# Keeping the weight chunks of the first token group in memory as they lie in their slots

## The reference

```
h  = rmsnorm(x) * g_mix
z  = h @ w_in                     # 512 pool | 512 q | 128 k | 128 v | 1024 gate_pool | 1024 gate_attn
A  = per-group map of (windowed mean - identity) of the pool part, scaled
B  = attention (8 heads, 2 kv heads, q and k normalised and rotated)
x += (sigmoid(gate_pool) * (A @ w_pool_out) + sigmoid(gate_attn) * (B @ w_attn_out)) @ w_out
h  = rmsnorm(x) * g_ffn
q  = h @ w_query                  # 8 heads, two halves of 128 each
s  = q . sub_keys                 # 128 scores per half; the best 16 of each half, merged to the best 16 pairs
x += sum over 8 heads x 16 experts of gelu(h . expert_u[id]) * gate * expert_v[id]
y  = rmsnorm(x) * g_final
```

## Time and profile before

| | |
|---|---|
| median of 3 runs | 2869.37 us (2869.11 to 2872.34) |
| the profiled execution: time, span | 2890.73 us, 2888.9 us |
| TensorE busy | 2606.0 us, 90% |
| VectorE busy | 2087.9 us, 72% |
| GpSimd busy | 1591.7 us, 55% |
| DMA moved | 965.76 MB, mean 334 GB/s |
| of it by gathers / by SP's queue | 671.17 MB / 261.61 MB |
| mean granted TensorE clock | 0.964 |

### The profile page before, as it was taken

The page is one execution under the profiler, slowest core; times in us unless marked ns, Lnnn a source line. Parts: engine busy times, 40 slices in busy tenths (PEclk is TensorE's granted clock), DMA queues, the critical chain, the costliest instruction groups (busy, mean ns, idle before and its releaser), DMA issues.

```text
span 2888.9 us, 30850 instructions
## 1 busy us (share of the span) xinstructions
PE 2606.0 (90%) x9957; PEld 1549.0 (54%) x9957; DVE 2087.9 (72%) x4622; ACT 538.5 (19%) x1205; POOL 1591.7 (55%) x1284
## 2 busy tenths in 40 slices
PE   7999958999798977999579999899999999999998
PEld 6867836885234455555344444455444545444454
DVE  1232987768707867788789987977777778777785
ACT  2141132221008104444430000010000000100001
POOL 0000165345765765344447877787777667666672
PEclk9999979999999989999899999999999999999999
DMA  4324599997898898899989999999999999999994
GB/s 160 103 84 131 200 328 338 388 326 260 324 372 289 299 368 290 281 346 311 328 311 405 412 376 414 411 376 412 413 413 413 414 413 413 414 413 413 410 410 190
DMA packets 345125, 965.76 MB, mean 334 GB/s; under 512 B 26018, under 2 KB 152738, under 8 KB 326306
## 3 DMA queue, kind: packets, MB, share of 16 engines
q0 software_dynamic: 184320, 671.17, 60.7%
q1 hardware_dynamic: 108800, 261.61, 24.2%
q10 hardware_dynamic: 51872, 31.46, 3.5%
HBM read 932.68 MB, written 31.46 MB: 334 GB/s over the span
## 4 chain that ended last, share of the span: by engine, by line
PE 32%; DMA 26%; DVE 22%; issue 12%; POOL 4%; ACT 3%; another core or an unknown queue 1%; DVEq 0%; ACTq 0%; POOLq 0%
DMA ring<-in_expert_v,idx 13%; PE bank L674 12%; DMA ring<-in_expert_u,idx 9%; PE bank L662 9%; DVE ring L1389 6%; POOL ring L1354 3%; PE bank L952 3%; PE o_bank L942 2%; PE o_bank L694 2%; DVE h L1389 2%; PE bank L733 2%; DVE region_c L1389 1%; DVE consts L1807 1%; DVE consts L1801 1%; DMA region_c<-in_expert_u,idx 1%
## 5 line engine op out<-in xcount | busy, mean ns | idle before, releaser
L1354 POOL DMA_INDIRECT ring<-in_expert_u,idx x468 | 608.3, 1300 | 667.3 <-DVE idx L1692 294.5
L952 PE MATMUL bank<-wslot,gate_attn 128*128 128x512 f32 x1536 | 697.8, 605 | 59.5 <-DVE gate_attn L1741 59.4
L1354 POOL DMA_INDIRECT ring<-in_expert_v,idx x428 | 507.5, 1186 | 323.2 <-issue 116.9
L942 PE MATMUL o_bank<-region_a,wslot 128*128 128x384 f32 x2048 | 681.3, 486 | 0.0
L942 PEld LDWEIGHTS o_bank<-region_a,wslot 128*128 128x128 f32 x2048 | 389.0, 190 | 298.0 <-issue 60.3
L952 PEld LDWEIGHTS bank<-wslot,gate_attn 128*128 128x128 f32 x1536 | 294.2, 193 | 420.5 <-issue 322.5
L1389 DVE CUSTOM_DVE_ANT_0 ring<-ring,h 128x1024 f32<-128x1024 f32 x380 | 451.5, 1222 | 48.4 <-DMA ring<-in_expert_u,idx 45.8
L1406 DVE SCALAR_TENSOR_TENSOR region_b<-ring,dots,region_b 128x1024 f32<-128x1024 f32 x256 | 328.6, 1283 | 120.8 <-DMA ring<-in_expert_v,idx 98.5
L1260 ACT ACTIVATE gate_attn<-o_bank 128x384 f32<-128x384 f32 x128 | 62.9, 491 | 1282.8 <-PE o_bank L942 1251.8
L674 PE MATMUL bank<-region_b,wslot 128*128 128x256 f32 (+1 forms) x768 | 231.6, 460 | 1.6 <-ACT region_b L989 1.6
L674 PE MATMUL bank<-region_a,wslot 128*128 128x256 f32 (+1 forms) x768 | 229.4, 457 | 2.9 <-DMA wslot<-in_w_in 1.7
(11 more groups left out here) (215 smaller groups left out, 2898.2 us busy)
## 6 DMA issues: line engine op xcount, KB each, us to landing
wslot<-in_expert_uT SPq DMA_DIRECT2D x64, 1024.0 KB
wslot<-in_expert_v SPq DMA_DIRECT2D x64, 1024.0 KB
wslot<-in_w_in SPq DMA_DIRECT2D x34, 1024.0 KB
wslot<-in_w_query SPq DMA_DIRECT2D x24, 1024.0 KB
expert_weights<-region_p ACTq DMA_DIRECT2D x24, 1024.0 KB
wslot<-in_w_out SPq DMA_DIRECT2D x12, 1024.0 KB
region_s<-expert_weights SPq DMA_DIRECT2D x8, 1536.0 KB
region_p<-expert_weights SPq DMA_DIRECT2D x8, 1536.0 KB, 12.8
```

The lines of the kernel that those rows point to most:

```text
L942: ins = nc.tensor.matmul(dense_in[q][:, 0:DENSE_T], u_cols[slot][:, k, :], mergeds[1][:, k, T - DENSE_T:T], start=(k == 0), stop=(k == KD ...
L952: ins = nc.tensor.matmul(dense_out[2 * t + n][:], hidden[q][:, t * P:(t + 1) * P], v_cols[slot][:, n * 512:(n + 1) * 512], start=start, st ...
L1354: nc.gpsimd.indirect_dma_start(ring_row(n), None, expert_u if what == "u" else expert_v, bass.IndirectOffsetOnAxis(ap=ids, axis=0)).then_i ...
```

## The change

Each of group 0's 29 chunks is stored to a DRAM tensor, `kept_dram`, from its slot, once it has landed there. The store of chunk m - 3 is issued on SP's queue right behind the load of chunk m (`STORE_BEHIND` is 3). The load that overwrites a slot (chunk m, where chunk m - 4 is of group 0) waits for that store too. The 53 chunks of groups 1 and 2 are loaded from `kept_dram`, where one partition's 8 KB lie in one run; their attn_out chunks take one DMA in place of two. `chunk_landed` counts accordingly and is moved up in the code. Nothing else is altered.

```diff
+KEPT = {chunk[1:]: n for n, chunk in enumerate(chunk_order(0))}
+STORE_BEHIND = WSLOTS - 1
...
+        kept_dram = nc.dram_tensor("kept_weights", (len(KEPT), P, KD * CHUNK), F32, kind="Internal").ap()
...
+        w_stored = sems("w_stored", WSLOTS)
...
+                count += 2 if n < len(KEPT) and CHUNKS[n][1] == "attn_out" else 1
...
+            def load_chunk(chunk):
+
+                m, name, c = CHUNKS.index(chunk), chunk[1], (chunk[2] if len(chunk) > 2 else 0)
+                dst, loaded = wslot[:, m % WSLOTS, :], w_loaded[m % WSLOTS]
+                if chunk[0]:
+                    sp.dma_start(dst, kept_dram[KEPT[chunk[1:]]]).then_inc(loaded, 16)
+                elif name in w_in_cols:
...
+            def keep_chunk(m):
+
+                chunk_landed(sp, CHUNKS[m])
+                sp.dma_start(kept_dram[m], wslot[:, m % WSLOTS, :]).then_inc(w_stored[m % WSLOTS], 16)
...
                     if m >= WSLOTS:
                         filled(sp, *LAST_JOB[CHUNKS[m - WSLOTS]])
+                        if m - WSLOTS < len(KEPT):
+                            sp.wait_ge(w_stored[m % WSLOTS], 16 * ((m - WSLOTS) // WSLOTS + 1))
...
+                    load_chunk(chunk)
...
+                    if STORE_BEHIND <= m < len(KEPT) + STORE_BEHIND:
+                        keep_chunk(m - STORE_BEHIND)
                     if name == "out" and c == 1 and g != LAST_GROUP[0]:
                         load_residual(g)
```

More of the change, by code:

```diff
@@ L504, in all_used, with chunk_landed @@
                 used(eng, n)
+        def chunk_landed(eng, chunk):
+            m = CHUNKS.index(chunk)
+            count = 0
+            for n in range(m % WSLOTS, m + 1, WSLOTS):
+                count += 2 if n < len(KEPT) and CHUNKS[n][1] == "attn_out" else 1
+            eng.wait_ge(w_loaded[m % WSLOTS], 16 * count)
+            return m % WSLOTS
         block = ctx.enter_context(nc.Block())
@@ L525, in load_residual @@
                                  res_loaded, 16)
+            w_in_cols = {"p": 0, "q": POOL_W, "kv": POOL_W + Q_W, "gate_pool": POOL_W + QKV_W,
+                         "gate_attn": POOL_W + QKV_W + D}
+            def load_chunk(chunk):
[4 more added lines that the diff above has]
+                elif name in w_in_cols:
+                    at0 = w_in_cols[name] + c * CHUNK
+                    sp.dma_start(dst.rearrange("p (k n) -> p k n", k=KD),
+                                 w_in[:, at0:at0 + CHUNK].rearrange("(k p) n -> p k n", p=P)).then_inc(loaded, 16)
+                elif name == "pool_out":
+                    sp.dma_start(dst.rearrange("p (g n) -> p g n", g=GROUPS),
+                                 w_pool_out[:, c * 512:(c + 1) * 512].rearrange("(g p) n -> p g n", p=P)).then_inc(
+                                     loaded, 16)
+                elif name == "attn_out":
+                    dst = dst.rearrange("p (j n) -> p j n", j=PAIRS)
+                    for half in range(KV_HEADS):
+                        src = w_attn_out[half * PAIRS * HD:(half + 1) * PAIRS * HD,
+                                         c * 512:(c + 1) * 512].rearrange("(j p) n -> p j n", p=HD)
+                        sp.dma_start(dst[half * HD:(half + 1) * HD], src).then_inc(loaded, 16)
+                else:
+                    w = w_out if name == "out" else w_query
+                    sp.dma_start(dst.rearrange("p (k n) -> p k n", k=KD),
+                                 w[:, c * CHUNK:(c + 1) * CHUNK].rearrange("(k p) n -> p k n", p=P)).then_inc(loaded, 16)
+            def keep_chunk(m):
+                chunk_landed(sp, CHUNKS[m])
+                sp.dma_start(kept_dram[m], wslot[:, m % WSLOTS, :]).then_inc(w_stored[m % WSLOTS], 16)
             load_x(0)
@@ L529, in _ @@
             sp.dma_start(g_mix_sb[:], g_mix).then_inc(first_loaded, 16)
-            w_in_cols = {"p": 0, "q": POOL_W, "kv": POOL_W + Q_W, "gate_pool": POOL_W + QKV_W,
-                         "gate_attn": POOL_W + QKV_W + D}
             for g in range(len(GROUP_OF)):
@@ L624, in encoder_kernel @@
         FIRST_ALL, CONSTS_ALL = 2 * 16, 7 * 16
[L626 to L633, removed]
         @block.tensor
```

## The result

The changed kernel takes 2885.15 us (median of 6 runs, 2876.84 to 2888.61), the kernel before on the same chip 2870.86. One of the six executions of the kernel before took 5476.58 us; it is in this median and left out of the ratio. The ratio is 1.0048, with an interval of 1.0032 to 1.0064: 0.48% slower, about 14 us. Forecast were 2861 us and 0.28% faster.

What follows compares the result with a forecast made beforehand. TensorE was taken to bound the untouched last stage, half the time; gathers and VectorE's dots mattered earlier. Gains 1.5 + 4.8 + 0.6 + 1.0 + 0 + 0 = 7.9 us gave 2861 us, range 2856 to 2866 (8 in 10: 2846 to 2878).

Steps and rivals of the forecast that it cites:

- part 4: Group 0's 29 stores: 73 us of DMA time, mostly under an idle stretch, expected to cost 0.
- one turn: SP's chain in group 0 from load to next load: 7.9 us, 8.3 with keys, at most 9.7, against 9.1.
- the rival that I gave 9%: Slower by the stores: group 0's turn exceeds 9.1 us; at 10 us group 0 ends 14 us later, 2876; chance 9%.
- Part 1: Shorter DMA time of the 53 loads: a gather before group 1's attention comes 1.5 us earlier, bounds 0 and 2.4.
- part 2: Group 1's late chunks: waits around the first out chunk go; 4.8 us, then 0.6 and 1.0.
- two gathers' worth: Before group 1's out, loads draw about 1.2 MB forward, against 8 ring slots, so VectorE's dots don't get later.
- slower by the gathers: Loads' larger share delays gathers 1.6 us each; nine chunks in group 2 cost 14 us, giving 2876; chance 8%.
- The 0.6: In group 1, the wait for the second w_out chunk goes, winning 0.6 us.
- the 1.0 of the clock: Group 1's first out chunk runs faster after a shorter pause, winning 1.0 us (0 to 2.1).
- Part 3: Group 2's loads: no chunk is late, so 0; bounds 4 us won and 4 lost.
- the rival in which the loads have an equal share at 1 KB already: Bundled 1 KB runs leave only 1.5 us gained, 2868; a second way to nothing to be seen, together 26%.
- The last stage: Half of the kernel's time, bound by TensorE; the change touches none of it, so it stays 1413 us.

Runs made afterwards that it cites:

- after, once more: The changed kernel, unchanged, run again beside others on one chip for a second profile: 2909.24 us, ratio 1.0035.
- before, once more: The kernel before, unchanged, run again for a second profile: 2892.57 us.
- two behind: Changed kernel with STORE_BEHIND 2 in place of 3, so chunk m - 2 is stored behind load m: 2888.95 us, ratio 0.9979.
- stores alone: Changed kernel with its stores and waits, but groups 1 and 2 load from the old places in 1 KB runs: 2913.79 us, ratio 1.0056.
- stores alone two behind: Changed kernel with STORE_BEHIND 2 and groups 1 and 2 loading from the inputs in 1 KB runs: 2893.69 us, ratio 0.9993.
- small stores three behind: Changed kernel storing 1 KB of each partition's 8, STORE_BEHIND 3, groups 1 and 2 loading from the inputs: 2894.65 us, ratio 0.9997.
- Loads only: Changed kernel without stores or waits for them; the kept layout is an input laid out before the launch: 2889.94 us, ratio 0.9973.
- with 2 KB: Changed kernel without stores, the copy an input laid out so groups 1 and 2 load in 2 KB runs: 2861.78 us, ratio 0.997.
- group 1 alone: Changed kernel without stores, the copy an input; only group 1 loads from it, group 2 from the old places: 2891.28 us, ratio 0.997.
- all laid out: Changed kernel without stores; all 82 chunks, group 0's too, load from an input in slot layout, 8 KB runs: 2863.9 us, ratio 0.9962.
- the kernel with the moved residual: Kernel before with group 1's residual issued behind its first out chunk in place of ahead of it: 2874.53 us, ratio 1.0002.

## Why the prediction was wrong, point by point

**The step that failed** is part 4, "one turn". I put load, keys, store and end at 8.3 us, 9.7 at most, against a limit of 9.1, and booked zero although the upper bound was past the limit. After takes 9.9 a turn over sixteen turns. The terms, by after, once more:

- A turn without keys is 9.04 us (201.56 to 210.60), where I had 4.4 + 2.5 + 1 = 7.9. The two transfers take 7.5 us from first byte to last and 1.6 lies around them. I had 3.5 (126.25 to 129.8, the load's bytes in the earlier trace rows) + 2.5 = 6.0 for the bytes, counting the store at full rate behind a full load; the slow start and the dip at the hand-over come to the rest. Such a turn alone still fits the limit of 9.1, just.
- A turn with keys is 9.7 us, as the mean of the five from 249.36 to 297.87; I had 8.3. This is the bound, and past the limit.
- I left out what shares the queue and the engines. The residual makes one turn 11.56 us (228.70 to 240.26; it was issued behind store 15, ahead of this turn's load). The gathers begin in group 0's last 35 us, and there two turns take 15.26 and 10.76 (from 297.87 and 313.13).

Against 9.1 a turn, the residual's turn is 2.5 us over and the two beside the first gathers 7.8; the other thirteen come to 3.5. The sixteen turns of 9.96 so come to 14 us over the limit, three quarters of it from what I left out. The attention of group 1 ends 13.1 us later than before (457.2 and 444.1), 15.0 against before, once more, and 16.3 in the second pair. This is the rival that I gave 9%, with its own example: "at 10 us group 0 ends 14 us later, 2876". The example has 14 less 7.9, some 6 us above before; measured are 14 above, and the intervals of the parts are too wide to say where the rest lies. Shown by: two behind is faster than before, three behind slower; stores alone +0.56%, stores alone two behind nothing, small stores three behind nothing. That the turn is too long is thus shown by experiments; how its excess divides is read off one profile.

**Part 1 and part 2** were right in their sum, and that is in part luck. Loads only gives 0.27%, 7.8 us, and 7.9 was forecast; `out` starts 5.8 us earlier in the pair of profiles, against 6.3. But the terms were off in both directions. Group 1 starts at 331.7 and 331.5, and its attention ends 3.8 us earlier (442.2 and 438.4), not 1.5, and past the bound of 2.4. From there to `out` 2.0 us are won (50.0 and 48.1), not 4.8. The wait before `out` stays at 6.3 in place of 3.5: the "two gathers' worth" that the loads draw forward is not free, since VectorE waits 6.7 us for rows in 455:492 in loads only, and not at all there in before, once more. Part of my rival "slower by the gathers" is thus real, with 2.5 to 3.3 us in this place (6.27 and 7.02 with runs of 8 KB, 3.74 with 2 KB). The 0.6 and the 1.0 of the clock can't be seen in loads only: the four `out` chunks took 30.91 us, and 30.4 in before, once more; a pause of 6.3 us still stood ahead of them. With the pause of 3.74 they took 29.58.

**Part 3**: zero, as forecast (0.9970 with group 1 alone, 0.9973 with both).

**The packets**: about one for one with loads of 1, 2 and 8 KB. This rules out the rival in which the loads have an equal share at 1 KB already. It does not rule out bundles, as the prediction has it: engines that take as many descriptors from each queue at a turn would give the same counts. The Trainium skill describes packets of several descriptors ("DMA: Bandwidth & Descriptors", Queues, rings and completion order); no run here shows whether the turns go by one or by several.

**The last stage** took 1415.7 us in after (1465.6 to 2881.3) and 1412.9 in the second profile, with 1413 forecast.

**The sum.** Stores +0.56% and loads -0.27% make +0.29%; measured are +0.48% (0.32 to 0.64) and +0.35% (0.16 to 0.54). With 0.2% to either side of each term, the parts add up as far as can be told.

**What stays open.** The lateness at ids0 is 13 to 16 us, at gate2 2.8 in the first pair and 6.5 in the second, yet the time is 10 to 14 us longer. Stores only is 30 us late at gate2, at a cost of 16. Between gate2 and the last stage single profiles of one kernel scatter by more than that: the stage starts at 1465.6 and 1481.1 in the two of after. So where in groups 1 and 2 the lateness is made up for a while, and where it comes back, isn't shown.

**The best version** is all laid out, at 0.9962, level with loads only within the noise; it presumes the layout in memory before the launch. Of kernels that do it themselves, the changed one with stores two behind is the fastest tried, 0.9979.

## What to carry to other kernels

Where a load waits for a store that was issued behind the load before it, the turn is the sum of both, not the larger (9.04 us here): measure it whole, and compare it with the time in which the consumer uses a buffer, for the longest run of turns and with all that shares the queue. An upper bound that is past the limit is not a cost of zero; multiply it by the number of turns. Storing one chunk earlier (two behind in place of three) turned +0.35% into -0.21%.

Beside gathers of 4 KB the run length of a load set its share (0.26, 0.37 and 0.68 of the engines with 1, 2 and 8 KB), and the share had a price on the gathers: a medium run can be as good as the longest.

## What was unexpected on the hardware

A small wait costs more than itself. After waits of 1.91, 1.63, 3.26 and 4.25 us the next chunk of 32 matmuls took 8.86 us in place of 7.07 (the rows of after's timeline above; the one at 331.64 had no wait). The granted clock was 0.81 in 308:317, a mean that lies between its two levels, 1.2 GHz (0.5) and 2.4 GHz (1.0), and 1.00 in 331:338, the upper level throughout:

```profile
308.00:317.00 9.00, 8.55 (x32) 7.24 (x33) 8.76 (x34) 0.38 (x1) 0.00 (x0) 0.81 1.01 401
...
331.00:338.00 7.00, 6.97 (x35) 6.16 (x35) 6.90 (x31) 1.19 (x4) 0.00 (x0) 1.00 0.66 221
```

It isn't so each time: after 2.88 and 2.93 us in the kernel with the moved residual a chunk took 7.17, and so it did after 1.86 us in stores only (at 248.61). The length of the wait alone doesn't decide it; what does isn't shown.

A store of 1 MB issued right behind a load of 1 MB on a queue with nothing else landed 8.5 us after its issue. The bytes of both moved for 7.5 us, where by the rates of the earlier trace rows (3.16 us per MB in 230:300 and 2.41) they would be 1.05 x 3.16 + 1.05 x 2.41 = 5.8 us.
